# Probabilities and values split into two parts for one product a block, and the low parts of queries and keys moved to GpSimd

## The chip, the cores and the metric

The kernel runs on one core of one Trainium2 chip, in one launch. The metric is the device time of that core in microseconds (us), lower is better. Engines are named as in the profile: PE is TensorE, DVE is VectorE, ACT is ScalarE, POOL is GpSimd, SP is SyncE.

## The reference: what is computed

One layer for two inputs at once: a prompt of 1024 rows and eight single decode rows with 32 cached pages of 128 tokens each. The width is 1024, half of it attention (8 heads of 64), half a pooling mixer. All data are fp32. The part that the change touches is the attention of the prompt:

```
def block(i):                      # 128 queries at a time
    s = jnp.einsum('bqhd,bkhd->bhqk', q_blk, k) * scale
    s = s + (F_blk[..., :, None] - Fh[..., None, :])     # sums of the forget gates
    s = jnp.where(kpos[None, :] <= qpos[:, None], s, NEG_INF)
    p = jax.nn.softmax(s, axis=-1)
    return jnp.einsum('bhqk,bkhd->bqhd', p, v)
```

Before it stands the projection `x @ w_in` (queries, keys, values, forget gates, mixer input), behind it `w_o`, a layer norm, a gated MLP of width 2816 and a second layer norm. The decode rows score 8 x 32 pages of keys; two of the eight rows (the "early" ones) are scored during the attention of the prompt.

## The kernel before, in words

**fp32 products.** PE multiplies at full precision only slowly, so most products are made from parts: x = hi + lo, where hi is x rounded to the type F32R ("fp32r" in the profile) by a copy, and lo = x - hi. Three products, hi\*hi + hi\*lo + lo\*hi, stand for one (`PARTS`, L1205). The product of probabilities and values (L1278) is not split before: it is one plain fp32 product, which PE carries out as two matmul instructions.

**The attention stage.** Heads come in four pairs, a pair has two heads, a head has 8 query blocks: 64 slots `x`, slot `x` being step `s` = x mod 16 of pair `p`. Block i of a head has i + 1 key blocks. The engines run the same loop over slots, each in its own program order, and meet at semaphores. In slot x:

- PE: `scores(x)` into the one score buffer S (two banks), then a chunk of the projection of the next pair (`CHUNKS`, L1205), then the transposes of the probabilities of slot x-1 into the one buffer TB (L1218), a second chunk, and `weighted_values(x-2)` into the one bank OB (L1278). In step 1 the values of the pair are turned through TB, in step 11 the keys of the next one, in step 2 the finished rows of the pair before (`turn_pair`).
- DVE: maximum and bias (L1748) of slot x, which frees S; in steps 0, 1, 11, 12 and 13 the lo parts of queries and keys (L1631, L1637); reductions of early decode keys (L1654); in even slots the copy of the turned probabilities out of TB (L1791); the reciprocal of the sum (L1795); last the scaled rows of x-2 (L1809), which frees OB.
- ACT: the exponential of slot x (L989); in odd slots the copy out of TB (L1008); the projection results out of their banks (`keep`, L892); the hi parts of queries and keys (L902, L909); rows of keys and of a pair out of TB (L921, L930).
- POOL: the products of early keys with the query (`multiply`, L769), and lo parts of projection weights (L778).
- SP: loads. An early product is a buffer of two pages (256 KB each). `early_keys(n)` first waits until the reduction of the product that used the buffer (k_red) is done. The early products are numbered 0 to 31; `EMUL` gives the slot of each: 8, 8, 9, 10, 14, 15, 18, 18, 19, 20, 21, 22, 23, 23, 24, 25, 26, 30, 31, 34, 34, 35, 36, 37, 38, 39, 39, 40, 41, 42, 46, 47. `ERED` is one slot later: there DVE reduces it, the first of a slot ahead of the copy out of TB, a second one behind it, and there SP loads the product KE numbers later. SP takes these in program order too. The load at the start of a decode row is preceded by `queries(b)`, which waits for the products of the row before.

```
KE = 4
KE_SLOTS = [ACC[:, 2, :], ACC[:, 3, :], WR[:, 2, :], WR[:, 1, :]]
if ERED[n - KE] == x:
    if n % NKP == 0:
        queries(n // NKP)
    early_keys(n)
```

The order in which TB and OB change hands is fixed by lists of names (T and O); whoever fills the buffer waits (`claim_tb`, `claim_ob`) until the one before has been emptied. In O the two small query products of the decode rows, ("q", 0) and ("q", 1), stand right behind ("pv", 0) and ("pv", 2); PE makes them in slots 3 and 5 (L1304), directly behind the scores.

## Time and profile before

| | |
|---|---|
| median of 3 runs | 1396.32 us (1395.48 to 1396.6) |
| profiled execution | 1396.35 us, its span 1394.5 us |
| PE busy | 1343.7 us, 96% of the span |
| DVE, ACT, POOL busy | 693.9, 358.6, 548.5 us |
| start of the attention stage to its end | about 60 to 385 us |

A busy time is the union of an engine's instructions. "Idle before" is the time that an engine stood still ahead of an instruction, with the instruction that released it. A matmul's duration reaches past the start of the next one, so costs on PE are read from start to start.

### The profile page before, as it was taken

The page shows a single profiled execution, that of the slowest core. Times are in us where ns is not written, and L with a number is a line of the kernel's source. Part 1 is how long each engine was busy: PE and PEld are TensorE (multiplying, and loading weights), DVE is VectorE, ACT ScalarE, POOL GpSimd, SP SyncE. Part 2 cuts the span into 40 slices and gives each one's busy share as a digit, 9 for nine tenths or more (in the row PEclk, how much of TensorE's full clock was granted, in tenths as well). Part 3 has the DMA queues.
Part 4 walks back from the last instruction along what each step waited for, and adds up shares of the span by engine and source line. Part 5 has one row for each costly group of instructions (what it writes and reads, how often), then busy time and mean ns, then how long its engine had stood idle before and what let it go on. Part 6 is the DMA issues. An engine that isn't in the chain of part 4 may idle for free. (4 is left out here: it accounts for less than half of the span.)

```text
span 1394.5 us, 21289 instructions
## 1 busy us (share of the span) xinstructions
PE 1343.7 (96%) x7605; PEld 1078.8 (77%) x7605; DVE 693.9 (50%) x1038; ACT 358.6 (26%) x527; POOL 548.5 (39%) x262
## 2 busy tenths in 40 slices
PE   7899999999989899999999999999999999999997
PEld 5889999999869886677777777777777776666675
DVE  4745665653556583553546465544634334321327
ACT  3524444443341233112021202121210201111116
POOL 1014454704110036656575657566562212121114
PEclk9999999999989999999999999999999999999999
DMA  7334453511035216777777777778776445367533
GB/s 246 104 116 150 129 185 103 170 43 53 25 107 219 86 45 220 256 243 243 231 261 240 243 247 241 234 236 266 222 253 215 158 141 202 152 262 277 223 145 122
DMA packets 111769, 255.02 MB, mean 183 GB/s; under 512 B 12848, under 2 KB 22961, under 8 KB 106280
## 3 DMA queue, kind: packets, MB, share of 16 engines
q1 hardware_dynamic: 102384, 247.00, 53.0%
q10 hardware_dynamic: 8320, 4.19, 1.1%
q0 software_dynamic: 960, 2.47, 0.5%
q8 instruction: 60, 0.98, 0.3%
q14 instruction: 45, 0.37, 0.1%
HBM read 243.73 MB, written 10.12 MB: 182 GB/s over the span
## 5 line engine op out<-in xcount | busy, mean ns | idle before, releaser
L829 POOL TENSOR_TENSOR WL<-WR,WH 128x1024 fp32r<-128x1024 f32 x55 | 132.1, 2402 | 427.4 <-ACT WH L1051 427.4
L769 POOL TENSOR_TENSOR AR<-AR,QB 128x1024 f32<-128x1024 f32 x96 | 232.6, 2439 | 101.1 <-DMA AR<-cache_k 88.5
L1454 PE MATMUL PSM<-XH,WH 128*128 128x512 f32 x672 | 215.7, 402 | 0.0
L1454 PE MATMUL PSM<-XL,WH 128*128 128x512 f32 x672 | 210.7, 395 | 0.0
L1454 PE MATMUL PSM<-XH,WL 128*128 128x512 f32 x672 | 210.7, 394 | 0.0
L2029 DVE TENSOR_TENSOR ACC<-ACC,PSM 128x512 f32<-128x512 f32 x160 | 108.7, 684 | 141.6 <-PE PSM L1464 141.5
L1454 PEld LDWEIGHTS PSM<-XH,WH 128*128 128x128 f32 x672 | 121.9, 188 | 53.3 <-issue 27.6
L1051 ACT CAST WH<-WR 128x1024 fp32r<-128x1024 f32 x55 | 57.5, 1047 | 367.3 <-PE PSM L1454 189.5
L1454 PEld LDWEIGHTS PSM<-XH,WL 128*128 128x128 f32 x672 | 126.3, 188 | 29.9
L1454 PEld LDWEIGHTS PSM<-XL,WH 128*128 128x128 f32 x672 | 126.2, 188 | 29.6
L1464 PE MATMUL PSM<-R 128*128 128x512 f32 x528 | 148.5, 390 | 0.1
L1654 DVE TENSOR_REDUCE AR<-AR 128x16 f32<-128x1024 f32 x80 | 96.8, 1211 | 91.5 <-POOL AR L769 91.5
L1464 PE MATMUL PSM<-WH,R 128*128 128x512 f32 x352 | 140.6, 400 | 0.1
L1205 PE MATMUL PSM<-XH,WH 128*128 128x344 f32 x384 | 134.2, 350 | 5.7 <-DVE WL L1626 4.7
L1205 PE MATMUL PSM<-XH,WL 128*128 128x344 f32 x384 | 123.7, 322 | 0.0
L1205 PE MATMUL PSM<-XL,WH 128*128 128x344 f32 x384 | 123.5, 322 | 0.0
L1464 PEld LDWEIGHTS PSM<-R 128*128 128x128 f32 x528 | 99.0, 188 | 22.1 <-DVE R L2017 0.5
L989 ACT ACTIVATE AR<-AR,negm 128x128 f32<-128x128 f32 (+3 forms) x64 | 49.7, 777 | 157.0 <-DVE negm L1748 157.0
L1464 PEld LDWEIGHTS PSM<-WH,R 128*128 128x128 f32 x352 | 66.1, 188 | 29.3 <-issue 12.8
L1205 PEld LDWEIGHTS PSM<-XH,WH 128*128 128x128 f32 x384 | 73.4, 191 | 8.8 <-DVE WL L1626 5.5
L2010 DVE TENSOR_TENSOR AR<-AR,PSM 128x1024 f32<-128x1024 f32 x21 | 25.6, 1220 | 107.9 <-PE PSM L1454 102.0
L1205 PEld LDWEIGHTS PSM<-XL,WH 128*128 128x128 f32 x384 | 73.4, 191 | 0.7 <-issue 0.7
(266 smaller groups left out, 2144.3 us busy)
## 6 DMA issues: line engine op xcount, KB each, us to landing
AR<-cache_v SPq DMA_DIRECT2D x256, 256.0 KB, 3.3
AR<-cache_k SPq DMA_DIRECT2D x192, 256.0 KB, 3.5
AR<-ws SPq DMA_DIRECT2D x37, 1024.0 KB, 6.4
WR<-ffn SPq DMA_DIRECT2D x66, 512.0 KB, 4.8
WR<-w_in SPq DMA_DIRECT2D x20, 512.0 KB, 4.7
ACC<-cache_k SPq DMA_DIRECT2D x32, 256.0 KB, 3.0
WR<-cache_k SPq DMA_DIRECT2D x32, 256.0 KB, 3.0
WR<-w_o SPq DMA_DIRECT2D x5, 1024.0 KB, 4.9
```

The costliest lines, as they stand in the source:

```text
L769: pool.tensor_tensor(keys, keys, QB[:].rearrange("p (o n) -> p o n", o=1).to_broadcast([P, KP, AW]), ALU.mult).then_inc(k_mul, 1)
L829: pool.tensor_tensor(lo, WR[:, raw_weight(e), :], hi.bitcast(F32), ALU.subtract).then_inc(ffn_lo, 1)
L989: act.activation(L[x % 2][:, 0:w], L[x % 2][:, 0:w], ACT.Exp, scale=-1.0, bias=negm[:, x % 2:x % 2 + 1], accum_out=rsum[:, x % 2:x % 2 + 1 ...
L1051: act.copy(weight_slot(kind, f)[0], WR[:, raw_weight(e), :]).then_inc(ffn_hi, 1)
L1205: ins = pe.matmul(third(n, m), w[a][:, tile_slot(n), k * P:(k + 1) * P], x[b][:, k, m * TH:(m + 1) * TH], start=(k == 0 and (a, b) == PART ...
L1454: ins = pe.matmul(out[:, hc], (hi, lo)[a][:, k * P:(k + 1) * P], x[b][:, k, hc], start=(k == 0 and n == 0), stop=(k == KC - 1 and n == 2))
L1464: ins = pe.matmul(PSM[:, 2 + n % 4, :], R2[:, 2 * r + a, i * P:(i + 1) * P], w[b][:, half * HALF:(half + 1) * HALF], start=(r == 0 and m = ...
L1654: dve.tensor_reduce(out[:, c * KP:(c + 1) * KP, :].rearrange("p j h -> p (j h)"), keys.rearrange("p (a n) -> p a n", n=HD), AX.X, ALU.add) ...
L2010: dve.tensor_tensor(GU, GU, PSM[:, 2:4, :].rearrange("p a n -> p (a n)"), ALU.mult).then_inc(gu_done, 1)
L2029: dve.tensor_tensor(cols, cols, PSM[:, 2 + n % 4, :], ALU.add).then_inc(d_free, 1)
```

## The change

The product of probabilities and values is made in F32R. The 128 turned probabilities of a key block stand beside each other as hi and lo (`split_rows`, 256 columns), and the values as hi and lo of 64 columns each (`VHL`), so that one matmul of 128x256 gives all products of parts. The result is transposed: rows are dimensions, columns are queries. DVE adds the three quadrants that count and multiplies by the reciprocals, which PE has turned and spread to 64 rows beforehand (`output_rows`). The result is already in the layout that `turn_pair` made, so `turn_pair` and `keep_pair` go; pair 0 alone is copied once (`keep_home`). Each slot's probabilities are now copied out of TB as hi by ACT, and then as lo by DVE. The values are turned in step 2 instead of 1, and leave TB through two copies of ACT (`value_rows`) and a subtraction of DVE. `query_lo` and `key_lo` of pairs 1 to 3 run on POOL. The new buffers take the place of two of the four early key buffers: KE is 2, and both are in WR. `output_rows(x-3)` runs in slot x right behind L1748, where the scaling of x-2 stood last in the slot. (The line numbers of the changed kernel differ: L1320 scores, L1261 projection, L1274 transposes, L1337 product, L1333 turned reciprocals, L1818 maximum and bias, L1853 lo of the probabilities, L1805 to L1807 output rows, L1705 key reductions, L787 early products, L793 and L800 lo of queries and keys.)

```diff
-KE = 4
+KE = 2
...
+        with nc.sbuf_tensor("SPLITW", [P, WS * D], F32R) as SPLITW:
+            pass
...
+        with nc.sbuf_tensor("SPLITA", [P, RT * D], F32R) as SPLITA:
+            pass
         ACC = sb("ACC", [P, RT, D])
+        with nc.sbuf_tensor("SPLIT", [P, 8 * D], F32R) as SPLIT:
+            pass
...
-        rinv = sb("rinv", [P, 2])
+        rinv = sb("rinv", [P, RT, 2])
...
-        PT = [AR[:, n * D:(n + 1) * D] for n in (2, 3)]
+        def split_rows(v):
+            if v % 2 == 0:
+                home = SPLIT[:, 2 * D:4 * D]
+            elif v < SLOTS - STEPS:
+                home = SPLITA[:, 4 * D:6 * D]
+            elif v < SLOTS - RT:
+                home = SPLITW[:, D:3 * D]
+            else:
+                home = R2[:, 0:2, :].rearrange("p a n -> p (a n)")
+            return home.rearrange("p (k a n) -> p k a n", k=RT, a=2)
...
-        AO = AR[:, 6 * D:7 * D]
+        VHL = SPLIT[:, 6 * D:8 * D].rearrange("p (k h a n) -> p k h a n", k=RT, h=2, a=2)
...
-        KE_SLOTS = [ACC[:, 2, :], ACC[:, 3, :], WR[:, 2, :], WR[:, 1, :]]
+        KE_SLOTS = [WR[:, 2, :], WR[:, 1, :]]
...
+        HOME = [ACC[:, 7, :], ACC[:, 1, :], ACC[:, 2, :], ACC[:, 3, :]]
...
-            torder += [("vn", p)] if s == 1 and p < PAIRS else []
-            torder += [("ct", p - 1)] if s == 2 and p >= 1 else []
+            torder += [("vn", p)] if s == 2 and p < PAIRS else []
...
+            def query_lo(p, hh):
+                a, b = slice(64 * hh, 64 * hh + 64), slice(64 - 64 * hh, 128 - 64 * hh)
+                pool.wait_ge(conv_hi, 6 * p + 3 * hh + 1)
+                pool.tensor_tensor(R2[b, 3 * hh, :], QX[a, :], R2[a, 3 * hh, :].bitcast(F32), ALU.subtract
+                                  ).then_inc(conv_lo, 1)
+                pool.wait_ge(conv_lo, 6 * p + 3 * hh + 1)
+            def key_lo(p, hh, n):
+                a, b = slice(64 * hh, 64 * hh + 64), slice(64 - 64 * hh, 128 - 64 * hh)
+                pool.wait_ge(conv_hi, 6 * p + 3 * hh + 2)
+                pool.tensor_tensor(R2[(a, b)[n], 3 * hh + 2, :], KX[p % 2][a, :], R2[a, 3 * hh + 1, :].bitcast(F32),
+                                  ALU.subtract).then_inc(conv_lo, 1)
+                pool.wait_ge(conv_lo, 6 * p + 3 * hh + 2 + n)
...
+                if s in (0, 1) and 1 <= p < PAIRS or s in (11, 12, 13) and p + 1 < PAIRS:
+                    pool.wait_ge(k_mul, sum(at < x for at in EMUL))
+                    pool.wait_ge(ent_lo, KC + 2 * WS + sum(ENTRY[n] + 1 < x for n in range(2 * WS, NWT)))
+                if s == 11 and p + 1 < PAIRS:
+                    query_lo(p + 1, 0)
+                if s in (12, 13) and p + 1 < PAIRS:
+                    key_lo(p + 1, 0, s - 12)
+                if s == 0 and 1 <= p < PAIRS:
+                    query_lo(p, 1)
+                if s == 1 and 1 <= p < PAIRS:
+                    key_lo(p, 1, 0)
+                    key_lo(p, 1, 1)
...
+            def value_rows(p):
+                act.wait_ge(tb_full, T["vn", p] + 1)
+                if p >= 1:
+                    act.wait_ge(ob_full, O["pv", STEPS * p - 1] + 1)
+                act.wait_ge(kn_st, 16 * (p + 1))
+                act.copy(VHL.rearrange("p k h a n -> p (k h) a n")[:, :, 0, :], TB.rearrange("p (k n) -> p k n", n=HD))
+                act.copy(VN, TB).then_inc(vn_kept, 1)
...
+            def keep_home(p):
+                act.wait_ge(ob_free, O["pv", STEPS * p + STEPS - 1] + 1)
+                act.wait_ge(g_st, 16 * NB)
+                act.copy(ACC[:, p, :], HOME[p]).then_inc(home_done, 1)
...
-                if 0 <= v < SLOTS and v % 2:
-                    w = (v % RT + 1) * P
+                if 0 <= v < SLOTS:
+                    n = v % RT + 1
                     act.wait_ge(tb_full, T["t", v] + 1)
                     if v >= 2:
                         act.wait_ge(ob_full, O["pv", v - 2] + 1)
-                    act.copy(PT[1][:, 0:w], TB[:, 0:w]).then_inc(tb_free, 1)
+                    if v == SLOTS - STEPS + 1:
+                        act.wait_ge(k_red, EARLY)
+                    act.copy(split_rows(v)[:, 0:n, 0, :], TB[:, 0:n * P].rearrange("p (k n) -> p k n", n=P)).then_inc(pt_hi, 1)
                 if x < SLOTS:
...
             def weighted_values(v):
-                p, s = divmod(v, STEPS)
-                hh, i = s // RT, s % RT
-                ob = claim_ob(O["pv", v])
+                p, at = divmod(v, STEPS)
+                hh, i = at // RT, at % RT
+                claim_ob(O["pv", v])
+                pe.wait_ge(inv_done, v + 1)
+                pe.transpose(OB[0:HD, 2 * P:3 * P], rinv[:, i, hh:hh + 1].to_broadcast([P, HD]), ident[:])
                 pe.wait_ge(tb_free, T["t", v] + 1)
                 pe.wait_ge(tb_free, T["vn", p] + 1)
                 for kt in range(i + 1):
-                    ins = pe.matmul(ob[:, 0:HD], PT[v % 2][:, kt * P:(kt + 1) * P],
-                                    VN[p % 2][:, kt * P + hh * HD:kt * P + hh * HD + HD],
-                                    start=(kt == 0), stop=(kt == i))
+                    ins = pe.matmul(OB[:, 0:2 * P], VHL[:, kt, hh].rearrange("p a n -> p (a n)"),
+                                    split_rows(v)[:, kt].rearrange("p a n -> p (a n)"), start=(kt == 0), stop=(kt == i))
                 ins.then_inc(ob_full, 1)
-
-            def turn_pair(p):
-                claim_tb(T["ct", p])
-                pe.wait_ge(ob_free, O["pv", STEPS * p + STEPS - 1] + 1)
-                turn(lambda i: AO[:, i * P:(i + 1) * P]).then_inc(tb_full, 1)
             def mixer(g):
...
+            def output_rows(v):
+                q, r = divmod(v, STEPS)
+                hh, i = r // RT, r % RT
+                rows, dims = slice(i * P, (i + 1) * P), slice(64 * hh, 64 * hh + HD)
+                dve.wait_ge(ob_full, O["pv", v] + 1)
+                if v == 0:
+                    dve.wait_ge(conv_lo, 6)
+                    dve.wait_ge(tb_free, T["kn", 0] + 1)
+                elif r == 0 and q == 1:
+                    dve.wait_ge(g_st, 16 * NB)
+                elif r == 0 and q == PAIRS - 1:
+                    dve.wait_ge(conv_lo, 6 * PAIRS)
+                    dve.wait_ge(tb_full, T["kn", PAIRS - 1] + 1)
+                out = HOME[q][dims, rows]
+                link(dve.tensor_reduce(out, OB[0:HD, 0:2 * P].rearrange("p (a n) -> p n a", a=2), AX.X, ALU.add))
+                link(dve.tensor_tensor(out, out, OB[HD:P, 0:P], ALU.add))
+                dve.tensor_tensor(out, out, OB[0:HD, 2 * P:3 * P], ALU.mult).then_inc(ob_free, 1)
...
-                if s == 11 and p + 1 < PAIRS:
-                    query_lo(p + 1, 0)
-                if s in (12, 13) and p + 1 < PAIRS:
-                    key_lo(p + 1, 0, s - 12)
-                if s == 0 and 1 <= p < PAIRS:
-                    query_lo(p, 1)
-                if s == 1 and 1 <= p < PAIRS:
-                    key_lo(p, 1, 0)
-                    key_lo(p, 1, 1)
...
+                if x >= 3:
+                    output_rows(x - 3)
...
-                if s == 1 and p < PAIRS:
-                    dve.wait_ge(tb_full, T["vn", p] + 1)
-                    if p >= 2:
-                        dve.wait_ge(vn_st, 16 * (p - 1))
-                    dve.tensor_copy(VN[p % 2], TB).then_inc(tb_free, 1)
+                if s == 2 and p < PAIRS:
+                    dve.wait_ge(vn_kept, p + 1)
+                    parts = VHL.rearrange("p k h a n -> p (k h) a n")
+                    dve.tensor_tensor(parts[:, :, 1, :], TB.rearrange("p (k n) -> p k n", n=HD),
+                                      parts[:, :, 0, :].bitcast(F32), ALU.subtract).then_inc(tb_free, 1)
                 v = x - 1
                 if 0 <= v < SLOTS:
-                    if v % 2 == 0:
-                        w = (v % RT + 1) * P
-                        dve.wait_ge(tb_full, T["t", v] + 1)
-                        if v >= 2:
-                            dve.wait_ge(ob_full, O["pv", v - 2] + 1)
-                        dve.tensor_copy(PT[0][:, 0:w], TB[:, 0:w]).then_inc(tb_free, 1)
+                    q, r = divmod(v, STEPS)
+                    hh, i = r // RT, r % RT
+                    dve.wait_ge(pt_hi, v + 1)
+                    part = split_rows(v)
+                    dve.tensor_tensor(part[:, 0:i + 1, 1, :], TB[:, 0:(i + 1) * P].rearrange("p (k n) -> p k n", n=P),
+                                      part[:, 0:i + 1, 0, :].bitcast(F32), ALU.subtract).then_inc(tb_free, 1)
                     dve.wait_ge(e_done, v + 1)
-                    if v >= 2:
-                        dve.wait_ge(ob_free, O["pv", v - 2] + 1)
...
-                    dve.tensor_scalar(AO[:, i * P + hh * HD:i * P + hh * HD + HD], OB[:, 0:HD],
-                                      rinv[:, v % 2:v % 2 + 1], None, ALU.mult).then_inc(ob_free, 1)
```

On PE, from the end of slot 8 over slot 9 to the start of slot 10 (steps 8 to 10 of pair 0), before: PSM is any bank, R the queries and keys, AR the working buffers.

```order
L1278 MATMUL PSM<-AR 128x64 x7
L1264 MATMUL PSM<-R 128x256 x2
L1268 MATMUL PSM<-causalR,identR 128x128
...
L1205 MATMUL PSM<-XH,WL 128x344
L1218 MATMUL PSM<-ident_sb,AR 128x128
L1205 MATMUL PSM<-XH,WH 128x344
...
L1278 MATMUL PSM<-AR 128x64 x8
L1264 MATMUL PSM<-R 128x384 x2
```

The same place in the changed kernel, SPLIT and SPLITA being the split probabilities and values:

```order
L1333 MATMUL PSM<-ident_sb,rinv 64x128
L1337 MATMUL PSM<-SPLIT 128x256 x7
L1320 MATMUL PSM<-R 128x256 x2
L1324 MATMUL PSM<-causalR,identR 128x128
...
L1261 MATMUL PSM<-XH,WL 128x344
L1274 MATMUL PSM<-ident_sb,AR 128x128
L1261 MATMUL PSM<-XH,WH 128x344
...
L1333 MATMUL PSM<-ident_sb,rinv 64x128
L1337 MATMUL PSM<-SPLITA,SPLIT 128x256 x8
```

Each block has the same place and count (the x7 and x8 are blocks), with one small matmul more ahead of them.

On DVE, slot 22 (step 6 of pair 1), before:

```order
L1748 ISA AR,negm<-PSM,AR 128x896
L1748 ISA negm 128x1
L1654 TENSOR_REDUCE PR<-WR 128x16
L1795 RECIPROCAL rinv<-rsum 128x1
L1809 TENSOR_SCALAR AR<-PSM,rinv 128x64
```

And in the changed kernel:

```order
L1818 ISA AR,negm<-PSM,AR 128x896
L1818 ISA negm 128x1
L1805 TENSOR_REDUCE ACC<-PSM 64x128
L1806 TENSOR_TENSOR ACC<-ACC,PSM 64x128
L1807 TENSOR_TENSOR ACC<-ACC,PSM 64x128
L1705 TENSOR_REDUCE PR<-WR 128x16
L1853 TENSOR_TENSOR SPLITA<-PSM,SPLITA 128x6x128
L1856 RECIPROCAL rinv<-rsum 128x1
```

One instruction at the end of the slot has become three ahead of the key reduction, and every slot, not each second one, has an instruction that empties TB.

On POOL, from the first early products (slot 8) on, before and then after; WR and ACC are the key buffers, R2 the queries and keys:

```order
L769 TENSOR_TENSOR ACC<-ACC,QB 128x1024 x2
L769 TENSOR_TENSOR WR<-WR,QB 128x1024
L778 TENSOR_TENSOR WL<-WR,WH 128x1024
L769 TENSOR_TENSOR WR<-WR,QB 128x1024
L769 TENSOR_TENSOR ACC<-ACC,QB 128x1024 x2
```

```order
L787 TENSOR_TENSOR WR<-WR,QB 128x1024 x3
L810 TENSOR_TENSOR WL<-WR,WH 128x1024
L787 TENSOR_TENSOR WR<-WR,QB 128x1024
L793 TENSOR_TENSOR R2<-ACC,R2 64x1024
L800 TENSOR_TENSOR R2<-ACC,R2 64x1024 x2
L787 TENSOR_TENSOR WR<-WR,QB 128x1024 x2
L793 TENSOR_TENSOR R2<-ACC,R2 64x1024
```

The lo parts of queries and keys now stand between the early products, all of which use WR.

## Rows read from the trace of the kernel before

**Rows 1.** The page: busy us (share) xinstructions of each engine.
```profile
PE 1343.7 (96%) x7605; PEld 1078.8 (77%) x7605; DVE 693.9 (50%) x1038; ACT 358.6 (26%) x527; POOL 548.5 (39%) x262
```
**Rows 2.** Windows: length, then busy us of each engine, granted clock, DMA share, GB/s.
```profile
60.00:385.00 325.00, 313.26 (x2213) 298.96 (x2213) 182.17 (x368) 129.00 (x250) 125.56 (x70) 0.99 0.35 112
```
**Rows 3.** Timeline of PE and ACT, 305.7 to 308.3 us: start, us, instruction.
```profile
305.85 1.89 PE L1278 MATMUL PSM<-ACC,AR 128*128 128x64 f32 x16
...
307.56 0.60 PE L1264 MATMUL PSM<-R 128*128 128x384 f32 x2
```
**Rows 4.** Timeline of PE behind the attention, products with w_o.
```profile
408.33 0.28 PE L1402 MATMUL PSM<-WH,XH 128*128 128x256 f32 x1
408.45 0.28 PE L1402 MATMUL PSM<-WL,XH 128*128 128x256 f32 x1
```
**Rows 5.** Timeline of slots 3 and 18: PE, turned rows and query products.
```profile
76.87 3.66 PE L1304 MATMUL PSM<-WR,SC 128*8 128x128 f32 x32
...
157.19 1.06 PE L1218 MATMUL PSM<-ident_sb,AR 128*128 128x128 f32 x8
...
158.00 0.40 PE L1205 MATMUL PSM<-XH,WH 128*128 128x344 f32 x1
```
**Rows 6.** Groups of instructions, 60 to 390 us: busy us, mean ns | idle before <-releaser.
```profile
L1809 DVE TENSOR_SCALAR AR<-PSM,rinv 128x64 f32<-128x64 f32 x64 | 18.2, 284 | 98.5 <-PE PSM L1278 98.0
L1637 DVE TENSOR_TENSOR R<-ACC,R 64x1024 fp32r<-64x1024 f32 x13 | 15.8, 1219 | 0.3
L1631 DVE TENSOR_TENSOR R<-ACC,R 64x1024 fp32r<-64x1024 f32 x6 | 10.3, 1725 | 0.2
L989 ACT ACTIVATE AR<-AR,negm 128x1024 f32<-128x1024 f32 x8 | 9.2, 1152 | 23.2 <-DVE negm L1748 23.2
L1748 DVE CUSTOM_DVE_ANT_0 AR<-PSM,AR 128x256 f32<-128x256 f32 x8 | 3.4, 425 | 1.7 <-PE PSM L1268 1.2
L1008 ACT COPY AR<-PSM 128x1024 f32<-128x1024 f32 x8 | 8.1, 1015 | 8.8 <-PE PSM L1218 8.8
```
**Rows 7.** Timeline of DVE, steps 6 and 7 of pair 2.
```profile
248.90 1.09 DVE L1748 CUSTOM_DVE_ANT_0 AR<-PSM,AR 128x896 f32<-128x896 f32 x1 [0.65 <-PE PSM L1268]
...
253.15 1.23 DVE L1748 CUSTOM_DVE_ANT_0 AR<-PSM,AR 128x1024 f32<-128x1024 f32 x1 [0.76 <-PE PSM L1268]
...
254.29 1.22 DVE L1654 TENSOR_REDUCE PDN<-ACC 128x16 f32<-128x1024 f32 x1
255.43 1.08 DVE L1791 COPY AR<-PSM 128x896 f32<-128x896 f32 x1
```
**Rows 8.** One early product: DVE and SP timelines, landings of L484, POOL timeline.
```profile
162.72 1.22 DVE L1654 TENSOR_REDUCE PR<-WR 128x16 f32<-128x1024 f32 x1
...
164.12 3.49 SPq L484 DMA_DIRECT2D WR<-cache_k  x4
...
DMA to landing us min/median/max: 2.6/3.0/5.1
...
269.50 2.39 POOL L769 TENSOR_TENSOR ACC<-ACC,QB 128x1024 f32<-128x1024 f32 x1
```
**Rows 9.** Waits of PE in 60 to 400 us: total, times, longest.
```profile
PE PSM L1218 <- DVE AR L1783: 3.3, 2, 1.9
PE PSM L1218 <- ACT AR L921: 2.2, 3, 0.7
PE PSM L1218 <- DVE ACC L1783: 1.9, 1, 1.9
```
**Rows 10.** Timeline of DVE and POOL, step 11 of pair 2.
```profile
271.85 5.71 POOL L769 TENSOR_TENSOR WR<-WR,QB 128x1024 f32<-128x1024 f32 x2
271.94 3.35 DVE L1631 TENSOR_TENSOR R<-ACC,R 64x1024 fp32r<-64x1024 f32 x1
```
**Rows 11.** Timeline of PE at the end of the stage.
```profile
387.89 1.78 PE L1218 MATMUL PSM<-ident_sb,AR 128*128 128x128 f32 x8 [0.47 <-DVE AR L1809]
390.87 1.87 PE L1353 MATMUL PSM<-ident_sb,SC 128*8 128x128 f32 x8 [1.19 <-ACT ACC L930]
```

115 lines of the change are left out of this document (50 added, 65 removed).

## The prediction

> **What bounds the kernel now.** The page first: TensorE is busy for 96% of the span, the Vector engine for half of it [rows 1]. An average hides stages, so the windows come next: in the 325 us of the attention stage TensorE is busy for 313 us at a granted clock of 0.99, that is at 2.4 GHz; the Vector engine has 182 us of work, ScalarE 129, GpSimd 126 [rows 2]. So TensorE sets the pace there, and what the change does to its instructions counts in full, as long as the others keep up. The groups show who waits: the Vector engine stood still for 98 us ahead of its scaled rows, always for the product on TensorE [rows 6]. The list of TensorE's own waits is short: the copy of the values out of the turning buffer held it for 5.2 us, the copy of the keys for 2.2 us [rows 9]. Nothing behind the stage changes, so I take it to move with the end of the stage.
>
> **What TensorE saves.** Four pairs of two heads with 36 blocks are 288 blocks. 16 matmuls of the plain fp32 product, two a block, take 1.71 us from the first to the next instruction (305.85 to 307.56): 0.107 us each, 0.214 us a block [rows 3]. A 128x256 F32R matmul with new weights each time, the form that the block gets now, starts 0.118 us after the one before [rows 4]. 288 x (0.214 - 0.118) = **27.6 us saved**. Eight turned tiles take 0.81 us (157.19 to 158.00), 0.10 each [rows 5]; the turned reciprocals are 64 more of these: **6.5 us added**. Three `turn_pair` inside the stage go: **2.5 us saved**. The fourth stands at the end: turn, wait for ScalarE's copy, and only then the next turn, 387.89 to 390.87 [rows 11]. These 3.0 us go, with the 0.5 us wait for the scaled rows ahead of them; some of it comes back, because the last probabilities leave the buffer in two steps: **3 us saved**. Together 26.6 us.
>
> The Trainium skill, "FP8 and Floating Point Precision", section "TensorE Precision Notes", counts true fp32 as four passes. By that rule 64 fp32 columns cost as much as 256 F32R columns and the first term would be zero. The trace has 0.214 against 0.118 us [rows 3, 4]; I go by it.
>
> **What the other engines get.** Vector engine: three linked instructions in place of the 0.284 us row scaling. 64x256 read, then 64x128 twice, each behind its forerunner's end: from 3 x 0.284 = 0.85 us to 3 x 0.425 and two gaps of 0.1 = 1.5 us [rows 6]; I take 1.1, nearer to the small form since two of the three have 128 elements. 64 x (1.1 - 0.28) = 52 us. The copy out of the turning buffer comes in every slot and not in each second: 32 more of about 0.8 us, 26 us. Away go 6 query and 12 key parts, 6 x 1.72 + 12 x 1.22 = 25 us [rows 6]. 182 + 53 = 235 us of some 315: 75% busy, not the bound on average. ScalarE gets 32 copies of about 0.7 us and eight of 1.0, some 30 us on 129 [rows 2, 6]: no bound either. GpSimd gets 18 instructions on 64 rows: between 1.2 us (the Vector engine's own) and 2.4 us (its early product) [rows 6, 8]; with 2.4 that is 43 us on 126. They are due by step 8 or the next pair, many microseconds later, so I cost them at nothing; if that cover were gone each would hold up the scores by its 2.4 us.
>
> A product of GpSimd and a query part of the Vector engine, both with two inputs in SBUF, stood in each other's way: 3.35 us instead of 1.22 [rows 10]. The pair is gone in the changed kernel, since the Vector engine's new instructions have one input in PSUM. The Trainium skill, "SBUF — State Buffer", section "Summary: rules for kernel authors", says that the later of such two waits until the first ends, and only if the Vector instruction has two SBUF inputs; this trace agrees, and if it held for the new instructions as well each of them could wait up to 2.4 us.
>
> **What holds TensorE up anew.** Four places.
>
> *The ring of early keys* has two buffers and no longer four. One turn: reduction ends (162.72 + 1.22), first load issued at 164.12, the second page 0.5 us later, landing 3.0, GpSimd 2.4, reduction 1.2: 7.4 us, so with two buffers one product in 3.7 us at best [rows 8]. The order asks for eleven products in the nine slots from step 2 to 10 of pairs 1 and 2. A slot is now some 3.9 us: 4.25 us from step 6 to 7 [rows 7], less five blocks of 0.096, plus 0.1. Eleven times 3.7 is 41 us, nine slots are 35: the last reduction is 6 us late. The Vector engine waits for a key ahead of the instruction that frees the turning buffer, so TensorE stops behind it; it can be up to one slot ahead, of which some 1.5 us is left. That is 4.5 us in each of the two runs and 2 us in the first (four products in slots 8 to 10): **11 us lost**. Ends: nothing, if the lead covers it all, and 16 if a turn is 4 us (a landing takes up to 5.1 [rows 8]).
>
> *The values* now pass two ScalarE copies (1.0 us each) and then a subtraction of 1.2 us before the buffer is free. ScalarE begins after its exponential, 2.1 us into step 2, so the buffer is free at 5.4; TensorE has turned the values (0.9), made one chunk of the projection and stands at 2.7. Four times 2.7 = 11 us. The old waits for the values, 5.2 us, go [rows 9], as does ScalarE's copy of the finished pair in step 2, and the engine restarts cost a few tenths each: **3 us lost** net; ends -2 and 6.
>
> *The one product bank.* The query products of the decode rows in slots 3 and 5 (L1304, 3.66 us [rows 5]) follow directly on the scores and need rows 0 and rows 2 out of the bank. Before, these were scaled at the end of the slot before; now they come behind L1748 of the same slot. TensorE waits for L1748 (0.6 and 0.8 us, behind scores that end at once) and 1.1 us of output rows: 1.8 + 2.1, **4 us lost**.
>
> *Full-width slots.* In step 7, L1748 (1.23), exponential (1.15 and 0.19), hi copy (0.9), lo (1.0) form a chain of 4.7 us with its gaps, to the next L1748 [rows 6, 7], against a slot of about 4.1. It is made good in the next, narrow slot, but not where a key reduction (1.14 us from 254.29 to 255.43) comes on top: **1 us lost**, and 1 more in slot 4, where the gate transposes wait for 1.1 us of output rows.
>
> Sum: -26.6 + 11 + 3 + 4 + 2 = -6.6. The profiled execution took 1396.35 us (span 1394.5 and 1.85 around it), the median of three is 1396.32: **1390 us**.
>
> **Rivals.**
> 1. *The ring is hidden.* For it: TensorE's lead, and that a late reduction only matters once it passes that lead. Against: lateness adds up over nine slots, and rows 8 leave little to cut. 11 us less: 1379.
> 2. *The Vector engine sets the pace* (slower than before). Place: slots 9 to 48 with a key reduction. L1748 1.14, rows, reduction 1.14, lo 1.0, reciprocal 0.1: 4.5 us with rows at 1.1, 4.9 with 1.5, against TensorE's 4.1 in step 7 and 3.9 in steps 5 and 6. If rows or the split writes cost 0.5 us more than I take, the 27 such slots give 13 us: 1403. It decides from 0.25 us more a slot, where my 6.6 us are gone. For it: three dependent instructions out of PSUM that the trace has none of. Against: the narrow steps have 1 to 2 us to spare.
> 3. *No saving on TensorE*: the new block takes 0.214 us too, since its moving half reads split buffers. 27.6 us more, 1418. Rows 4 speak against it. The page on fp32 named above would give the same.
> 4. *The ring costs double*, because SP takes loads, projection weights and the query of the next row in order: 22 us, 1401.
>
> **Chances and numbers.** My forecast 0.47 (own range 1384 to 1396), the hidden ring 0.22, the Vector engine 0.18, the double ring 0.09, no saving 0.02, the rest for something unseen. 0.2% is 2.8 us, about what a measurement of this kernel tells from no change. Faster takes nearly all of the first two, less the forecast's upper edge: 0.64; the same 0.15 (edges of the forecast and of rivals 2 and 4); slower 0.21. The range 1376 to 1403 holds the forecast and rivals 1, 2 and 4.
>
> **What would show it.** Right: the product has 288 matmuls some 0.118 us apart; `turn_pair` is gone; the Vector engine is busy for about 235 us in the stage and waits for GpSimd's products, 10 us or more, with steps 3 to 11 of pairs 1 and 2 longer than their work; TensorE's waits name the copy of the values, about 11 us, and the output rows in slots 3 and 5. Wrong: no wait for GpSimd (rival 1), a Vector engine without gaps in steps 4 to 7 (rival 2), output rows far from 1.1 us, or a drop of the granted clock in the stage after waits of 2 to 3 us, which the waits before (up to 1.9 us [rows 9]) did not bring.

## The result, and the profile after

The changed kernel takes **1405.03 us** (median of four runs, 1402.33 to 1405.99) against 1396.26 us for the kernel before: ratio 1.0062, 95% interval 1.0046 to 1.0078. It is slower by 8.8 us, 0.6%, clear of the noise; 1390 us was forecast, with a range up to 1403. The profiled execution took 1405.53 us (span 1403.7).

The page's busy times, and the window that answers to [rows 2]:

```profile
PE 1328.9 (95%) x7349; PEld 1054.9 (75%) x7349; DVE 735.0 (52%) x1180; ACT 379.0 (27%) x564; POOL 591.9 (42%) x280
```
```profile
60.00:385.00 325.00, 291.74 (x1914) 269.89 (x1914) 212.88 (x489) 146.29 (x281) 165.35 (x85) 0.96 0.34 108
```

TensorE has 15 us less to do in the whole kernel and still ends later. In the 325 us it now stands idle for 33 us, where it had 12, and the mean granted clock fell from 0.99 to 0.96. Its waits, and those of the Vector engine and GpSimd (engine, line and tile that waited, what ended the wait; us in total, times, longest), 60 to 388 us:

```profile
POOL WR L787 <- DMA WR<-cache_k: 42.4, 16, 8.7
...
DVE PDN L1705 <- POOL WR L787: 11.8, 6, 4.1
...
DVE PR L1705 <- POOL WR L787: 10.7, 8, 2.8
PE PSM L1274 <- DVE SPLIT L1845: 9.8, 4, 2.6
...
PE PSM L1274 <- DVE SPLITA L1853: 8.1, 5, 2.6
...
PE PSM L1357 <- DVE ACC L1807: 3.8, 2, 2.0
...
PE PSM L1333 <- DVE ACC L1807: 3.3, 12, 1.1
```

All three chains of the forecast are there. GpSimd waits 42 us for pages of keys, the Vector engine 22.5 us for GpSimd's products, and TensorE stands behind the lo part of the probabilities (L1853) that the Vector engine owes it. The values' lo part (L1845) holds TensorE four times for up to 2.65 us, 9.8 us in all, where 11 were forecast. The last two lines are the one product bank: the query products (L1357) wait 3.8 us for output rows, and the turned reciprocals (L1333), which open the next product, another 3.3 us in twelve short waits.

The output rows by groups, and the new product: a product of five blocks, then the next scores.

```profile
L1805 DVE TENSOR_REDUCE ACC<-PSM 64x128 f32<-64x256 f32 x60 | 24.9, 414 | 0.9
L1806 DVE TENSOR_TENSOR ACC<-ACC,PSM 64x128 f32<-64x128 f32 x60 | 17.5, 291 | 2.1
L1807 DVE TENSOR_TENSOR ACC<-ACC,PSM 64x128 f32<-64x128 f32 x60 | 16.9, 281 | 2.0
```
```profile
301.87 0.83 PE L1337 MATMUL PSM<-SPLIT 128*128 128x256 f32 x5
302.53 1.08 PE L1320 MATMUL PSM<-R 128*128 128x512 f32 x4
```

0.414 + 0.291 + 0.281 us and the gaps are 1.05 us a slot (1.1 forecast). Five blocks take 0.66 us from first to next instruction, 0.13 each with the start of the group.

**Where the time went, slot by slot.** I cut both traces at the first scores of each of the 64 slots. Slot 63 starts at 387.47 us instead of 377.13, 10.3 us later; behind it some 1.1 us come back. Summed over the slots, from TensorE's start to start: products and scores -21.9 us, reciprocals +3.1, turned tiles -2.1; the rest is standing still or going slowly. Placed by slot, net of what was saved there: steps 1 and 2 of the four pairs +8.9 us, ring stalls in slots 11, 21, 25, 27, 28, 37 and 41 to 43 +14.7, query products +3.9, slot 4 +0.8, full-width slots (the last two of each head, steps 6, 7, 14 and 15) +3.9.

**The clock.** One thing has no counterpart before, where between 70 and 385 us the clock was at its upper level throughout. The window of the kernel before (the last three columns are granted clock, DMA share, GB/s), PE in step 2 of pair 1 of the changed kernel, then windows of the changed kernel:

```profile
70.00:385.00 315.00, 304.66 (x2174) 290.54 (x2172) 174.34 (x357) 125.69 (x243) 125.56 (x70) 1.00 0.34 110
```

```profile
163.72 0.32 PE L1261 MATMUL PSM<-XH,WL 128*128 128x344 f32 x1
166.69 0.69 PE L1274 MATMUL PSM<-ident_sb,AR 128*128 128x128 f32 x2 [2.65 <-DVE SPLIT L1845]
...
168.04 0.49 PE L1261 MATMUL PSM<-XH,WH 128*128 128x344 f32 x1
168.33 0.49 PE L1261 MATMUL PSM<-XL,WH 128*128 128x344 f32 x1
```
```profile
77.00:80.50 3.50, 3.49 (x14) 3.36 (x15) 0.49 (x2) 0.82 (x2) 0.00 (x0) 0.57 0.00 0
...
132.00:135.50 3.50, 3.50 (x14) 3.14 (x13) 2.12 (x5) 2.13 (x6) 3.42 (x2) 0.51 0.94 297
...
166.70:169.70 3.00, 3.00 (x11) 2.94 (x12) 0.49 (x2) 0.82 (x2) 1.88 (x1) 0.51 0.00 0
169.70:172.00 2.30, 2.30 (x17) 2.19 (x16) 1.30 (x4) 0.61 (x1) 0.00 (x0) 1.00 0.00 0
...
323.50:326.50 3.00, 3.00 (x12) 3.00 (x12) 0.49 (x2) 0.37 (x1) 0.00 (x0) 0.50 0.00 0
```

Ahead of 163.9 us the projection's matmuls start 0.16 us apart, behind the gap of 2.65 us they start 0.29 us apart: the granted clock is 0.5, that is 1.2 GHz, for some three microseconds, with TensorE fully busy. Between 70 and 385 us it happens five times, each time at a gap: 2.33, 2.56, 2.65, 2.65 and 2.18 us. Busy time times missing clock is 1.70 + 1.71 + 1.46 + 1.58 + 1.63 = **8.1 us**. Gaps of 1.76, 2.03, 1.90 and 2.08 us in the same trace were not followed by a fall.

**The clock behind the stage.** There the two profiled executions differ too. First the kernel before, then the changed one:

```profile
388.00:401.70 13.70, 10.64 (x40) 6.43 (x39) 6.53 (x14) 3.08 (x5) 1.47 (x3) 0.50 0.24 80
```
```profile
388.00:401.70 13.70, 9.76 (x60) 8.21 (x60) 9.01 (x20) 6.56 (x12) 2.21 (x3) 0.88 0.42 154
```

Part of the 1.1 us that come back at the end may be this, and not the change: the kernel before ran there at the lower level for 13.7 us, the changed one for 3.4.

### The profile page after: what moved, and what is told of

Same layout as the page of the kernel before. It is cut to its first block and busy times, and to the rows that moved or that the text cites. A ratio compares the mean times of both kernels' runs of the same rounds, so it can differ in the third digit from the quotient of the medians.

```text
span 1403.7 us, 20941 instructions
## 1 busy us (share of the span) xinstructions
PE 1328.9 (95%) x7349; PEld 1054.9 (75%) x7349; DVE 735.0 (52%) x1180; ACT 379.0 (27%) x564; POOL 591.9 (42%) x280
## 5 line engine op out<-in xcount | busy, mean ns | idle before, releaser
L787 POOL TENSOR_TENSOR AR<-AR,QB 128x1024 f32<-128x1024 f32 x96 | 231.4, 2427 | 91.5 <-DMA AR<-cache_k 79.0
L1504 PEld LDWEIGHTS PSM<-XH,WH 128*128 128x128 f32 x672 | 121.9, 188 | 53.4 <-issue 27.6
L1504 PEld LDWEIGHTS PSM<-XL,WH 128*128 128x128 f32 x672 | 126.2, 188 | 29.7
L1261 PE MATMUL PSM<-XH,WH 128*128 128x344 f32 x384 | 136.9, 356 | 5.9 <-DVE WL L1676 5.2
L1705 DVE TENSOR_REDUCE AR<-AR 128x16 f32<-128x1024 f32 x80 | 96.7, 1211 | 87.1 <-POOL AR L787 87.0
L1261 PE MATMUL PSM<-XH,WL 128*128 128x344 f32 x384 | 126.1, 328 | 0.0
L1261 PE MATMUL PSM<-XL,WH 128*128 128x344 f32 x384 | 126.1, 328 | 0.0
L787 POOL TENSOR_TENSOR WR<-WR,QB 128x1024 f32<-128x1024 f32 x32 | 75.9, 2384 | 49.0 <-DMA WR<-cache_k 42.4
L1261 PEld LDWEIGHTS PSM<-XH,WH 128*128 128x128 f32 x384 | 75.3, 196 | 9.0 <-DVE WL L1676 5.9
```

Of the source, the lines that this page charges most:

```text
L787: pool.tensor_tensor(keys, keys, QB[:].rearrange("p (o n) -> p o n", o=1).to_broadcast([P, KP, AW]), ALU.mult).then_inc(k_mul, 1)
L1261: ins = pe.matmul(third(n, m), w[a][:, tile_slot(n), k * P:(k + 1) * P], x[b][:, k, m * TH:(m + 1) * TH], start=(k == 0 and (a, b) == PART ...
L1504: ins = pe.matmul(out[:, hc], (hi, lo)[a][:, k * P:(k + 1) * P], x[b][:, k, hc], start=(k == 0 and n == 0), stop=(k == KC - 1 and n == 2))
L1705: dve.tensor_reduce(out[:, c * KP:(c + 1) * KP, :].rearrange("p j h -> p (j h)"), keys.rearrange("p (a n) -> p a n", n=HD), AX.X, ALU.add) ...
```

## The experiments

Each line gives the median, the kernel before measured beside it, the ratio of the two with its 95% interval, and "against", in us. For a kernel made from the changed one (a_...) this is the difference to the changed kernel: its ratio less 1.0062, times 1396 us. For one made from the kernel before (b_...) it is the difference to that kernel: its ratio less 1, times 1396 us. The intervals make such a difference uncertain by 1.3 to 4 us to either side (at 95%); a_queries and a_warm are not clear of noise. Three dots in a diff stand for further lines.

| kernel | median | before | ratio | against |
|---|---|---|---|---|
| b_pool_lo | 1387.79 | 1395.99 | 0.9933 [0.9908, 0.9958] | -9.4 |
| b_ring2 | 1402.95 | 1395.99 | 1.0047 [1.0035, 1.006] | +6.6 |
| b_lo_ring2 | 1394.2 | 1396.35 | 0.9978 [0.9965, 0.9991] | -3.1 |
| b_lo4_dve | 1388.71 | 1396.75 | 0.9942 [0.9926, 0.9959] | -8.1 |
| b_lo2_dve | 1394.7 | 1396.75 | 0.999 [0.998, 0.9999] | -1.4 |
| a_dve_lo | 1418.37 | 1395.99 | 1.0158 [1.0135, 1.0181] | +13.4 |
| a_noload | 1388.41 | 1395.99 | 0.9938 [0.9916, 0.9961] | -17.3 |
| a_step2 | 1396.2 | 1394.94 | 1.0004 [0.9996, 1.0013] | -8.1 |
| a_queries | 1402.46 | 1394.94 | 1.0046 [1.0034, 1.0058] | -2.2 |
| a_redlate | 1411.75 | 1394.94 | 1.0116 [1.0103, 1.0129] | +7.5 |
| a_ring3 | 1393.54 | 1394.94 | 0.9989 [0.9978, 1.0] | -10.2 |
| a_spread | 1392.61 | 1396.35 | 0.9965 [0.9946, 0.9983] | -13.5 |
| a_three | 1382.32 | 1396.35 | 0.9901 [0.9886, 0.9915] | -22.5 |
| a_floor | 1375.71 | 1396.35 | 0.9849 [0.9832, 0.9866] | -29.7 |
| a_warm | 1404.16 | 1396.75 | 1.0059 [1.0045, 1.0074] | -0.4 |
| a_best | 1379.79 | 1396.75 | 0.9885 [0.987, 0.99] | -24.7 |
| a_outfirst | 1421.1 | 1397.07 | 1.0183 [1.0158, 1.0207] | +16.9 |
| a_best_out | 1398.4 | 1397.07 | 1.0008 [0.9991, 1.0025] | +17.2 over a_best |

### The three parts of the change, one at a time

**b_pool_lo**: the kernel before, with nothing but the lo parts moved to GpSimd.
```diff
-                if s == 11 and p + 1 < PAIRS:
-                    query_lo(p + 1, 0)
...
+            def query_lo(p, hh):
...
+                pool.tensor_tensor(R2[b, 3 * hh, :], QX[a, :], R2[a, 3 * hh, :].bitcast(F32), ALU.subtract
+                                  ).then_inc(conv_lo, 1)
...
```


> The kernel before with only the lo parts of queries and keys of pairs 1 to 3 moved to GpSimd, ring of four. In step 1 the copy of the values stood behind two key parts of 1.2 us each on the Vector engine, and TensorE waited 2.0, 2.0 and 1.6 us there. Theory A: these 5.7 us go, GpSimd is in time everywhere: 1391 us (1389 to 1394). Theory B (GpSimd is late with them or with the early products behind them, so that the move costs): 1396 to 1400.

Measured: 9.4 us less by the median (5.9 to 12.9 by the interval), where theory A gave 5.7. TensorE's waits in it, 60 to 400 us:

```profile
PE PSM L1227 <- DVE WL L1648: 4.2, 1, 4.2
PE PSM L1240 <- ACT AR L943: 2.2, 3, 0.7
```

The waits for the values' copy [rows 9] are gone with the parts that stood ahead of it: slots 17, 33 and 49 are 1.96, 1.97 and 1.61 us shorter. That is 5.5 us, as theory A had it, and all that the trace shows of the move inside the stage. Most of the other 3.6 us between the two profiled executions lies elsewhere: the first scores start 1.0 us earlier, slot 0 is 0.45 us shorter, and behind slot 63 it is 1.8 us quicker, where the clock was at its lower level for 6.8 us and not for 13.7. The forecast had the gain of the three slots, but booked it under "the values".

**b_ring2**: the kernel before, with nothing but two buffers.
```diff
-KE = 4
+KE = 2
...
-        KE_SLOTS = [ACC[:, 2, :], ACC[:, 3, :], WR[:, 2, :], WR[:, 1, :]]
+        KE_SLOTS = [WR[:, 2, :], WR[:, 1, :]]
...
```


> The kernel before with only the ring of early keys cut from four buffers to two (both in WR); nothing else. Theory A (the 19 us that TensorE saves in the changed kernel are given back in waits, the ring of two being the largest with 14 to 15 us): here the slots are longer (4.2 instead of 3.9 us) and eleven products at 3.7 us want 41 us in nine slots of 38, so part of the wait shows already: 1397 to 1404 us, likeliest 1400, with the Vector engine waiting for GpSimd in steps 3 to 11 of pairs 1 and 2. Theory B (the Vector engine's added work is what costs, the ring is a bystander): within 1 us of 1396.

Measured: 6.6 us more, with an unusual scatter (1395.58 to 1405.53 us). The profile fell on the quickest of its ten executions, as quick as the kernel before, and the ring's cost is in it all the same. Slot 63 starts 4.7 us after that of the kernel before, relative to the first scores 4.9 us; slots 11, 22, 27, 28 and 38 are 0.3 to 1.4 us longer. Slots 17 and 18 are 2.9 us longer, because here the clock fell behind a wait of 1.87 us:

```profile
152.16 0.33 PE L1216 MATMUL PSM<-ident_sb,AR 128*128 128x128 f32 x1 [1.87 <-DVE AR L1781]
```
```profile
152.90:159.80 6.90, 6.90 (x32) 6.90 (x31) 1.04 (x5) 0.41 (x1) 2.83 (x2) 0.51 0.01 2
```

The kernel before has the same wait in the same place (1.9 us [rows 9]) with the clock up behind it. Behind slot 63 this execution is 5.4 us quicker than the kernel before, and the clock stays up where it fell there at 388 us. So some microseconds of each profiled execution are the clock's, and not the kernel's.

**a_dve_lo**: the changed kernel, with the lo parts back on the Vector engine.
```diff
+                if s == 11 and p + 1 < PAIRS:
+                    first_query_lo(0, p + 1)
+                if s in (12, 13) and p + 1 < PAIRS:
+                    first_key_lo(0, s - 12, p + 1)
...
```


> The changed kernel with the lo parts of queries and keys of pairs 1 to 3 back on the Vector engine. 18 instructions, 25 us of work, come back there, and GpSimd's early products wait for them again. Theory A: the Vector engine has room in steps 0, 1, 12 and 13, so +1 to +6 us: 1406 to 1411. Theory B (its work sets the pace): most of the 25 us show, 1420 or more.

Measured: 13.4 us more; both theories missed it. By slots, 2.1 us are lost in each of slots 17 and 33, and 0.8 to 1.3 in slots 12, 13, 28, 29 and 43 to 45, the steps where the parts stand. By these slots they cost the new kernel 12 us and the old one 5.5, though they are the same instructions; the medians, 13.4 and 9.4, are too uncertain to tell the two apart. The trace names the wait. The parts stand ahead of the output rows in the Vector engine's order, and TensorE, ahead of the turned reciprocals, waits until these are out of the one product bank, 60 to 388 us:

```profile
PE PSM L1325 <- DVE ACC L1799: 15.0, 21, 1.9
```

In the changed kernel the same wait (L1333 <- L1807) is 3.3 us in twelve; the 11.7 us more lie mostly in the slots named.

**a_noload**: the changed kernel; only the first two pairs of pages of early keys are loaded, and the other 30 products are made again from the same two tiles, so the decode scores are not those of the reference.
```diff
                         if n % NKP == 0:
                             queries(n // NKP)
-                        early_keys(n)
...
-                    pool.wait_ge(ke_ld[n % KE], 16 * KP * (n // KE + 1))
+                    pool.wait_ge(ke_ld[n % KE], 16 * KP)
+                    if n >= KE:
+                        pool.wait_ge(k_red, n - KE + 1)
```


> The changed kernel, in which only the first two early key products are loaded; the other 30 are made again from the same two buffers, so the scores of the two early decode rows are not those of the reference. GpSimd waits for the reduction two products back, but for no load. A turn of the ring is 3.6 us instead of 7.4. Theory A: the ring's 14 to 15 us go: 1388 to 1393 us. Theory B: the Vector engine keeps its instructions, so 1402 to 1405.

Measured: 17.3 us less. Theory B, the Vector engine alone, falls. By slots the ring's places are 15.1 us shorter; the rest is the clock, which fell twice between 70 and 380 us in this execution and not five times. But the ring costs the new products 17 us and cost the old ones 6.6; this gap became a question of its own.

**b_lo_ring2**: the kernel before with both side parts and without the main one (both diffs above).

> The kernel before with both side parts of the change and without its main one: the lo parts on GpSimd and two buffers of early keys. Theory A (the ring's cost is its own, and adds): 1387.8 + 6.6 = 1394.4 us; the main part, the products of split halves, then costs 10 us of its own, through the stalls of step 2, the product bank and the clock. Rival E (the ring costs the changed kernel 16.6 us because GpSimd has the lo parts between the early products): 1387.8 + 16.6 = 1404 us, and the main part costs next to nothing.

Measured: 6.3 us over b_pool_lo. Theory A holds, rival E falls, and the split products, the main part, cost 1.0062 - 0.9978, **11.7 us of their own**, where their work on TensorE is some 21 us less. The Vector engine waits even longer for GpSimd in this kernel, and yet TensorE has no wait over 2 us behind it (waits of b_lo_ring2, 100 to 330 us):

```profile
DVE PDN L1674 <- POOL WR L767: 20.4, 8, 5.4
DVE PR L1674 <- POOL WR L767: 17.3, 8, 3.6
```

### The stalls, one at a time

**a_step2**: the second chunk of projections ahead of the transposes in step 2.
```diff
+                if s == 2 and x < SLOTS:
+                    for n, m, k in CHUNKS[p, 2 * s + 1]:
+                        product_step(n, m, k)
                 v = x - 1
                 if 0 <= v < SLOTS:
...
-                if x < SLOTS:
+                if x < SLOTS and s != 2:
                     for n, m, k in CHUNKS[p, 2 * s + 1]:
                         product_step(n, m, k)
```


> The changed kernel, with one swap in TensorE's order: in step 2 of each pair the second chunk of projections stands ahead of the transposes of the probabilities, so it runs while the values are split. TensorE's longest gap there is 2.33, 2.65, 2.65 and 2.18 us before those transposes, and the chunk takes some 1.25 us at full clock. Theory A (only the gaps count): 4 x 1.25 us less, 1400 us. Theory C (the gaps also take the granted clock down: in the changed kernel it fell five times between 60 and 388 us, four of them right behind such a gap of step 2 (77, 166, 244, 323 us), each for some 3.5 us at half, 1.5 to 1.7 us lost each): 4 x (1.25 + 1.6) = 11.4 us less, 1393.5 us, and the granted clock of these four places 1.00. Theory B (Vector engine sets the pace of every slot): 1404 to 1405 us.

Measured: 8.1 us less, between theories A and C and over the 4.9 us by which the gaps became shorter. The projection of that slot now runs at full pace up to the wait, the gap is 1.24 us, and the scores that follow start on time:

```profile
161.48 0.31 PE L1261 MATMUL PSM<-XH,WL 128*128 128x344 f32 x1
163.03 0.44 PE L1274 MATMUL PSM<-ident_sb,AR 128*128 128x128 f32 x2 [1.24 <-DVE SPLIT L1848]
```

In its profile, which is its quickest execution and 3 us under the median, all four falls of step 2 are gone: slots 2, 18, 34 and 50 are 2.6, 2.7, 2.9 and 3.4 us shorter. One fall is left, from 78.7 us on, at the query products' wait of 1.81 us; slot 3 is 1.1 us longer for it.

**a_queries**: the query products behind the first chunk of projections of their slot.
```diff
-                if x in (3, 5):
-                    sample_queries((x - 3) // 2)
...
                     for n, m, k in CHUNKS[p, 2 * s]:
                         product_step(n, m, k)
+                if x in (3, 5):
+                    sample_queries((x - 3) // 2)
```


> The changed kernel, with the sample's query products of slots 3 and 5 behind the first chunk of projections of their slot instead of ahead of it, so that their wait for the one product bank lies behind other work. Theories A and C: the gaps of 1.76 and 2.03 us there go, 3.9 us less, 1401 us; no fall of the clock stood behind them. Theory B: no change, 1404 to 1405 us, since Vector engine has the same work in the same order.

Measured: 2.2 us less, not clear of noise by the medians. By slots, 3 and 5 are 0.9 and 0.7 us shorter. The wait ahead of these products falls from 1.76 and 2.03 to 0.77 and 0.20 us, but behind the second one the gate transposes now wait 1.64 us, where they waited 0.4.

**a_redlate**: each reduction of early keys at the end of its slot on the Vector engine.
```diff
-                for n in range(EARLY):
-                    if ERED[n] == x and EMUL.index(EMUL[n]) == n:
-                        reduce_keys(n)
...
-                    if ERED[n] == x and EMUL.index(EMUL[n]) != n:
+                    if ERED[n] == x:
```


> The changed kernel, with each reduction of early keys at the end of its slot on Vector engine, behind the lo parts of the probabilities, instead of ahead of them. Vector engine's 22 us of waits for GpSimd's products then stand behind the work that TensorE waits for in that slot; the loads are asked for some 3 us later. Theory A (the ring costs through Vector engine's queue): 8 to 12 us less, 1393 to 1397 us. Rival R (the ring's own round of load, product and reduction is longer than the slots between its uses, so that the loss comes back wherever the reduction stands): 1403 to 1409 us.

Measured: 7.5 us more. Theory A falls: the waits can't be moved behind the probabilities, since a later reduction asks later for the next pages. Rival R holds, a little over its range: the ring's round is the limit.

**a_ring3**: a third buffer, the tile of the third pair's output rows, as long as it is free.
```diff
+THREE = max(n for n in range(0, EARLY, 3) if ERED[n] <= 2 * STEPS + 2)
+EBUF = [n % 3 if n <= THREE else 1 + (n - THREE - 1) % 2 for n in range(EARLY)]
...
+        EB = [ACC[:, 2, :], WR[:, 2, :], WR[:, 1, :]]
...
```


> The changed kernel, with a third buffer of early keys (the tile that holds the third pair's output rows from slot 35 on) up to early product 18, two buffers from there on. Theories A and C: the ring's stalls of slots 11 to 28 go (3.5 + 2.4 + 1.25 + 1.05 + 1.7 = 9.9 us, with one fall of the clock in them), those of slots 37 to 43 stay: 1395 us. Rival (the 16.6 us that the kernel without loads gained come from the traffic of the loads, not from the count of buffers): 1403 to 1405 us.

Measured: 10.2 us less; slots 11, 21, 25, 27 and 28 are 3.5, 2.5, 1.3, 1.1 and 1.8 us shorter. 1.7 us of slot 11's are the fall of the clock at 132 us, which this execution does not have. The loads are the same in number and size, so it was the count of buffers.

**a_spread**: two buffers, no slot with two early products.
```diff
-ESLOTS = [x for x in range(8, 48) if x % STEPS not in (0, 1, 11, 12, 13)]
+ESLOTS = [x for x in range(8, 48) if x % STEPS not in (0, 1)]
```


> The changed kernel, with two buffers, and early products in steps 11 to 13 too, so that no slot has two of them. Theory A (the ring stalls where a slot has two products, or where products follow each other and the reductions come late): half of the 14.7 us of stalls goes, 1397 us. Rival (GpSimd's lo parts of steps 11 to 13 then come late for the scores of the next half): 1405 us or more.

Measured: 13.5 us less, by a table alone; a third buffer gave 10.2. The Vector engine's wait for GpSimd, 100 to 330 us, is 3.7 us in place of 22.5, and the wait of GpSimd for pages 29.1 in place of 42.4:

```profile
POOL WR L787 <- DMA WR<-cache_k: 29.1, 13, 8.2
...
DVE PDN L1705 <- POOL WR L787: 2.1, 4, 0.8
DVE PR L1705 <- POOL WR L787: 1.6, 2, 0.8
```

The lo parts of steps 11 to 13, which now share GpSimd with products, are not late by it: TensorE has no wait for them. Slots 14, 15, 31 and 47 grow by 0.8 to 1.0 us.

**a_three**: a_ring3, a_step2 and a_queries together.

> The changed kernel with the three mends together: third buffer up to early product 18, step 2's projections ahead of the transposes, query products behind the first chunk. If the gains of the single ones add (7.4 + 10.2 + 2.2 us, each from its ratio to the kernel before on its chip against the changed kernel's 1.0062): 1385 us. If the Vector engine's work sets a floor (theory B in its weak form), 1390 us or more. Kernel before with GpSimd's lo parts alone: 1387.8 us.

Measured: 1382.32 us; the single gains add up (20.5 us by the table, 22.5 measured).

**a_floor**: a_step2, a_queries and a_noload together, with the decode scores of a_noload.

> The changed kernel with step 2's projections ahead of the transposes and the query products behind the first chunk, and with the loads of all early keys but the first two left out (the products are made again from the two tiles, so the decode scores are not the reference's). It shows what the main part saves with no stall of the three kinds left: the kernel without loads had 1388.4 us, less 7.4 and 2.2 us: 1379 us if they add; 1386 us or more if another engine holds the slots.

Measured: 1375.71 us; they add as well (27.6 us by the table, 29.7 measured). With no early keys to wait for, 29.7 us come off the changed kernel.

### Two questions left open: the clock, and the ring's larger price

**a_warm**: 14 transposes of the identity into unused columns of the product bank keep TensorE busy in the gap of step 2.
```diff
+                if s == 2 and x < SLOTS:
+                    claim_ob(O["pv", x - 2])
+                    for _ in range(14):
+                        pe.transpose(OB[:, 3 * P:4 * P], ident[:], ident[:])
```


> The changed kernel with nothing moved and work added: in step 2 of each pair, where TensorE has its gap of 2.2 to 2.65 us, 14 transposes of the identity into unused columns of the product bank (about 1.8 us) keep it busy. Theory C (the gap takes the clock down for some 3.5 us at half): the falls behind step 2's gaps go, 3 or 4 x 1.6 = 5 to 6.5 us less, 1398 to 1400 us, though TensorE has 7 us more work. Theory A (only the gap's length counts): 1405 us, or some more where the added work reaches past the gap.

Measured: 1404.16 us; the difference to the changed kernel, -0.4 us, is uncertain by 3 us to either side. PE of a_warm in the same place, and its windows:

```profile
164.20 1.75 PE L1391 MATMUL PSM<-ident_sb 128*128 128x128 f32 x14
166.92 0.44 PE L1274 MATMUL PSM<-ident_sb,AR 128*128 128x128 f32 x2 [0.97 <-DVE SPLIT L1849]
...
167.67 0.32 PE L1261 MATMUL PSM<-XH,WH 128*128 128x344 f32 x1
167.83 0.32 PE L1261 MATMUL PSM<-XL,WH 128*128 128x344 f32 x1
```
```profile
77.00:80.50 3.50, 2.81 (x19) 2.29 (x17) 1.30 (x6) 0.82 (x2) 0.00 (x0) 1.00 0.00 0
98.50:101.50 3.00, 3.00 (x16) 1.95 (x15) 0.00 (x0) 0.00 (x0) 0.00 (x0) 0.50 0.00 0
132.00:135.50 3.50, 3.50 (x15) 3.22 (x15) 2.10 (x5) 2.13 (x5) 3.42 (x2) 0.54 0.86 289
166.70:169.70 3.00, 2.78 (x18) 2.65 (x19) 0.81 (x4) 0.82 (x2) 2.18 (x1) 1.00 0.03 5
...
258.50:261.50 3.00, 3.00 (x14) 2.79 (x13) 2.93 (x8) 1.61 (x3) 2.74 (x2) 0.51 0.51 165
```

In place theory C holds: all four falls of step 2 are gone, the same matmuls start 0.16 us apart, and these four slots are 1.2 to 1.5 us shorter. In total it misses: now the clock falls at 98.5 and 258.5 us, behind gaps of 2.03 and 2.07 us behind which it had stayed up, and it still falls at 132 us. Three falls of 1.7 us remain of five. The fall at 98 us is none of the added work's: a_noload, a_redlate and a_spread have it too, with their gap of step 2 unfilled and no fall behind it. Of the 5.5 us that the four slots give, it takes 1.7, and slots 25 to 43, where the ring stalls, take another 2.5, the fall at 258 us among it. So the falls are tied to gaps, but which gap is followed by one is not settled by its length and changes from execution to execution.

**b_lo4_dve** and **b_lo2_dve**: the old products with the lo parts on GpSimd, with four and with two buffers, and with the probabilities of every slot copied by the Vector engine, as in the changed kernel.
```diff
-                if 0 <= v < SLOTS and v % 2:
...
-                    act.copy(PT[1][:, 0:w], TB[:, 0:w]).then_inc(tb_free, 1)
...
-                    if v % 2 == 0:
...
-                        dve.tensor_copy(PT[0][:, 0:w], TB[:, 0:w]).then_inc(tb_free, 1)
...
+                    dve.tensor_copy(PT[v % 2][:, 0:w], TB[:, 0:w]).then_inc(tb_free, 1)
```


> The kernel before with GpSimd's lo parts and four buffers, and with Vector engine copying the probabilities of odd slots too (ScalarE did). It is the base for the next kernel: some 2 to 5 us over 1387.8 us, 1390 to 1393 us.

> As b_lo4_dve, with two buffers. Theory D (two buffers cost much where every slot's probabilities leave through Vector engine, behind its reductions that wait for GpSimd): 12 to 17 us over b_lo4_dve. Theory F (the coupling does not matter, and the ring's larger cost comes from something else in the new products): 6 to 7 us over it, as it was where ScalarE released every other slot.

Measured: 0.9942 and 0.999, 1388.71 and 1394.7 us; the ring costs 6.7 us here. Theory D falls: that every release goes through the Vector engine does not make the ring dear.

**a_outfirst**: the output rows ahead of the exponent's input on the Vector engine.
```diff
             for x, p, s in slots():
+                if x >= 3:
+                    output_rows(x - 3)
                 if x < SLOTS:
...
-                if x >= 3:
-                    output_rows(x - 3)
```


> The changed kernel with the output rows of the slot three back ahead of the exponent's input on Vector engine, instead of behind it: they then run while it waits for TensorE's scores (34 us of such waits between 60 and 388 us), and the product bank and the probabilities are released about 1 us sooner. Theory G (the row of work between a slot's scores and its probabilities is what the ring's lateness comes on top of): the full-width slots' 3.9 us, the query products' gaps (3.9 us) and 1 us of each of the ring's nine stalls go: 1392 us. Rival H (where Vector engine is late it has no idle time ahead of the scores, so that the exponents are only put off by 1 us and the order is worth nothing): 1403 to 1409 us.

Measured: 16.9 us more. Theory G falls; rival H had the direction right, but at most 4 us of it. The Vector engine in steps 6 to 8 of pair 1, first in the changed kernel, then in a_outfirst:

```profile
187.13 1.22 DVE L1705 TENSOR_REDUCE PR<-WR 128x16 f32<-128x1024 f32 x1 [0.16 <-POOL WR L787]
188.27 0.95 DVE L1853 TENSOR_TENSOR SPLITA<-PSM,SPLITA 128x768 fp32r<-128x768 f32 x1
...
189.21 1.20 DVE L1818 CUSTOM_DVE_ANT_0 AR<-PSM,AR 128x1024 f32<-128x1024 f32 x1
...
190.34 0.41 DVE L1805 TENSOR_REDUCE ACC<-PSM 64x128 f32<-64x256 f32 x1
...
191.31 1.21 DVE L1705 TENSOR_REDUCE PR<-WR 128x16 f32<-128x1024 f32 x1
192.52 1.09 DVE L1853 TENSOR_TENSOR SPLIT<-PSM,SPLIT 128x896 fp32r<-128x896 f32 x1
...
193.60 0.27 DVE L1818 CUSTOM_DVE_ANT_0 AR<-PSM,AR 128x128 f32<-128x128 f32 x1
```
```profile
187.31 1.21 DVE L1705 TENSOR_REDUCE PR<-WR 128x16 f32<-128x1024 f32 x1
189.28 0.96 DVE L1853 TENSOR_TENSOR SPLITA<-PSM,SPLITA 128x768 fp32r<-128x768 f32 x1 [0.76 <-ACT SPLITA L1067]
...
190.23 0.40 DVE L1805 TENSOR_REDUCE ACC<-PSM 64x128 f32<-64x256 f32 x1
...
191.19 1.21 DVE L1820 CUSTOM_DVE_ANT_0 AR<-PSM,AR 128x1024 f32<-128x1024 f32 x1
```

In the changed kernel the engine has no gap from 187.13 to 194.6 us: L1818, output rows, reduction and lo part are 4.39 us from 189.21 to 193.60, and TensorE's slot is 4.5. In a_outfirst the output rows, 0.96 us, stand between the reciprocal and the exponent's input; the hi copy comes later too, and the Vector engine waits 0.76 us for it ahead of its lo part: the move puts its idle time where it is lost. Over the stage, 60 to 388 us, TensorE's waits for lo parts of the probabilities (L1853) grow from 10.6 to 22.2 us. Slots 8, 15, 16, 24, 31, 32 and 40 are each 0.9 to 1.3 us longer; slots 3 and 5 gain 1.5 and 1.7, as theory G had it for the query products (0.3 us of slot 3's is the clock).

**a_best**: a_three with a_spread's table.

> The changed kernel with step 2's projections ahead of the transposes, query products behind the first chunk, third buffer up to early product 18, and early products in steps 11 to 13 too (none doubled). With three mends it took 1382.3 us; the stalls of two buffers behind slot 35 are what is left of the ring. If spreading takes half of them: 1379 us. If the lo parts of steps 11 to 13 come late by it: 1383 us or more.

Measured: **1379.79 us**, 0.9885 [0.987, 0.99], faster than both kernels and than b_pool_lo (0.9933). TensorE is busy for 300.56 of the 325 us, the clock stays up from 68 to 377 us:

```profile
60.00:385.00 325.00, 300.56 (x2013) 276.03 (x2013) 232.17 (x527) 154.12 (x295) 170.55 (x94) 0.98 0.37 118
```

**a_best_out**: a_best with a_outfirst's move.

> The fully mended kernel (1379.8 us) with the same move of the output rows. If they still stand in the way of the full-width slots there: 1376 us. If room is short only through the ring: 1379 to 1381 us. By rival H: 1382 us or more.

Measured: 1398.4 us, 17.2 us over a_best. The loss is the same with the ring's stalls mended, so it is not the ring's. By slots it lies mostly behind the full-width ones (8, 16, 24, 32, 40 and 48, 0.9 to 1.3 us each), in step 3 of pairs 1 and 2 (1.2 and 0.7 us) and in slots 56 and 62 (1.8 and 1.6). TensorE's waits for lo parts of the probabilities grow from 2.4 to 14.9 us, so it is again the chain of scores, exponent and split that becomes longer.

## Why the prediction was wrong

**What held.** TensorE's saving: products and scores -21.9 and reciprocals +3.1 make -18.8 us where 27.6 - 6.5 = 21.1 were forecast. That it is so close is partly luck: the saving was put 5.7 us too high, 3.5 of them because a block takes 0.13 us and not 0.118, and the reciprocals cost half of what was put down. The Trainium skill, "FP8 and Floating Point Precision", section "TensorE Precision Notes", counts true fp32 as four passes, by which the first term would be zero. The trace disagrees: a block went from 0.214 to 0.13 us. Turned tiles -2.1 (-2.5). Output rows 1.05 us (1.1). The gaps behind the values 9.8 us (11), the query products +3.9 (4), slot 4 +0.8 (1). The lo parts on GpSimd cost nothing, and b_pool_lo shows what they brought: 5.5 us in the three slots, where the forecast had 5.2, and 9.4 us by the median. The Vector engine has 213 us of work in the window, where 235 were forecast; it did not matter.

**The step that failed** is the pricing of the waits under "What holds TensorE up anew": every wait was taken at its length, and the work behind it at 2.4 GHz. A fall of the clock after waits of 2 to 3 us stood among the signs that would make the forecast wrong, but no term and no rival had it. In the profiled execution it came five times, four of them at the values' gaps, for 8.1 us. Of the 8.9 us of the steps 1 and 2, 6.4 are the clock; what is left, 2.5, is the 3 us forecast. The Trainium skill, "TensorE: Matmul & The Clock Gate", section "HAM oscillation — how this bites in real kernels", tells of idle stretches in mid-kernel, waits of some 3 to 5 us in its case, behind which the work runs at half the clock. This trace agrees in kind, but its falls stand at shorter waits, 2.2 to 2.65 us. a_step2 gains 8.1 us where the gaps' length gives 4.9. That the falls as such set the time is not shown: a_warm took four away, had two elsewhere and shows no gain in the median. Nor did the waits of up to 1.9 us stay without a fall in all executions, as the forecast's last sign assumed: b_ring2 has one of 6.9 us behind 1.87.

**Mis-sized terms.** The ring: 14.7 us by place (13 without the fall at 132 us) where 11 were forecast; 17.3 by a_noload's median, 15.1 by its slots. Its mechanism, two buffers and a round that is too long for the doubled slots, is shown from four sides (a_noload, a_redlate, a_ring3, a_spread). The full-width slots: 3.9 us where 1 was forecast. In slot 23, with a reduction, the Vector engine's queue is 4.39 us, so the products' 0.47 us come to nothing; this is the mechanism of rival 2, at less than a third of its price. But full-width slots without a reduction (7, 14, 30, 46) lose 0.3 to 0.4 us each as well. What TensorE waits for there is the product bank: the output rows of the product before are not out of it when the turned reciprocals come (L1333 <- L1807, 0.07 to 0.17 us in these slots, 0.24 in slot 23, and in slot 14 another 0.16 until the engine is going again). The forecast had this bank in slots 3 and 5 alone. The end: 1.1 us where 3 were forecast. TensorE waits 1.05 us for the last lo part and then 2.29 us, again for output rows in the one bank, which the forecast had not:

```profile
398.70 0.42 PE L1333 MATMUL PSM<-ident_sb,rinv 128*64 128x128 f32 x1 [2.29 <-DVE ACC L1807]
```

**The sum.** The profiled executions are 9.2 us apart, -6.6 was forecast, so 15.8 us are to be explained. The deviations are +8.1 (clock), +2 (ring), +2.9 (full width), +1.9 (end), +2.3 (work) and +0.4 (turned tiles), and 0.8 us the other way: 16.8. One microsecond is not assigned.

**By the experiments** the account is: lo parts -9.4, ring with the old products +6.3, main part +11.7. In the main part, -22 of work stands against step 2 (8.1, and 4 x 1.24 left), the query products (2.2, and 1.7 left), the full-width slots 3.9 and the ring's additional 11.0 (17.3 less 6.3): 31.9, or +10 net, where the runs gave 11.7.

**The rivals.** Rival 1, the hidden ring, put the ring at nothing and was wrong: it costs 17 us in the changed kernel and 6 in the old one. Rival 4 came close in time, 1401, but the ring's excess was 3.7 us by place and not 11, and its reason, SP's order, was not tried. Rival 3 was refuted by the products' pitch.

**What stays open.** Why the ring costs 11 us more beside the new products. It isn't GpSimd's lo parts (b_lo_ring2) and isn't that the Vector engine alone releases the probabilities (b_lo2_dve). A good part of it needs no cause in the Vector engine: where the ring's round sets the length of the slots, work that TensorE saves can't show. The traces bear this out for slots 19 to 28 and 35 to 44, measured together from first scores to first scores:

| | four buffers, or no loads | two buffers |
|---|---|---|
| old products | 87.2 us (b_pool_lo, b_lo4_dve) | 90.3 (b_lo_ring2), 92.7 (b_lo2_dve) |
| new products | 82.7 us (a_noload) | 94.5 (the changed kernel) |

The ring costs 3.1 and 5.5 us with the old products and 11.8 with the new ones. But 4.5 us of this are the work that the new products save in these slots and that two buffers don't let through; the changed kernel itself is only 1.8 to 4.2 us longer here than the old products with two buffers. For that rest, that the Vector engine's queue has less room, 212.9 us of work against 180.6 in b_lo2_dve, fits, but no run added that work to the old products alone.

## What to carry to other kernels

- Price a gap on TensorE by what follows it, too: look in the windows for the granted clock behind each wait of two microseconds and more, and move independent work into such a gap; here a swap of two blocks gave back 8 us, 5 of them by the gaps' length.
- When an engine's output gets a longer tail (two copies and a subtraction in place of one copy), ask of each buffer that it holds whether the next user stands directly behind. The saved work was real, 22 us; it only paid once the ring, the values and the query products were mended (a_three, a_best). And where a ring of buffers sets the pace, work saved on another engine does not show until the ring has room.
- A change in three parts should be tried in parts: one side part alone (b_pool_lo) made the kernel faster, while the sum made it slower.

## What the runs showed of the hardware

- The granted clock fell from 2.4 to 1.2 GHz at gaps of TensorE of 1.81 (a_step2 at 79 us) to 2.65 us: in the changed kernel five times for 3 to 4 us, each costing 1.4 to 1.7 us, and in b_ring2 at 152 us for 6.9 us, behind a gap of 1.87. In other executions it stayed up behind gaps of the same length: 2.65 us in a_noload at 164 us, 2.03 us in the changed kernel at 98 us, 1.87 us in the kernel before at 153 us. So two executions of one kernel may differ by a few microseconds: b_ring2's ten lie between 1395.58 and 1405.53 us.
- Eighteen Vector instructions of 1.22 to 1.73 us, 25 us in all, taken off an engine that was half idle, were worth 9.4 us by the median; 5.5 of them stand in the trace at three copies that had been queued behind these instructions. Put back into the changed kernel they cost 13.4 us.
- GpSimd needs 2.43 us for a difference on 64 partitions (two took 4.86 us from 158.98 us on), as long as for one on 128 (2.40 us at 156.44 us); the Vector engine needs 1.22 for 64 [rows 6].
